# Rotary halves exchanged by ScalarE copies into PSUM instead of signed-permutation matmuls, in a two-layer hybrid encoder

## The reference

```python
def apply_rope(t, cos, sin):
    t1, t2 = jnp.split(tf, 2, axis=-1)          # the two halves of each head, 32 + 32
    return jnp.concatenate([t1 * c - t2 * s, t2 * c + t1 * s], axis=-1)
...
for l in range(DEPTH):
    h = rmsnorm(x, attn_norm_g[l])
    q, k, v, conv_in, gate_logits = jnp.split(h @ w_in[l], SPLITS, axis=-1)
    q, k = apply_rope(q, cos, sin), apply_rope(k, cos, sin)
    y_attn = sliding_window_sink_attention(q, k, v, attn_sinks[l]) @ w_attn_o[l]
    u = causal_dwconv(ca * sigmoid(cb), conv_dw_w[l], conv_dw_b[l])   # width 31
    y_conv = silu(layernorm(u)) @ w_conv_o[l]
    x = x + (sigmoid(g_attn) * y_attn + sigmoid(g_conv) * y_conv) @ w_out[l]
    # then RMSNorm, up-projection, convolution of width 3, SiLU gate, down-projection
```

## Time and profile before

| what | value |
|---|---|
| median of 3 runs | 888.76 us (888.66 to 890.28) |
| profiled execution, its own time | 884.6 us |
| its span, from first to last instruction | 882.8 us |
| TensorE matmul busy | 850.5 us (96%) |
| VectorE busy | 627.9 us (71%) |
| ScalarE busy | 473.2 us (54%) |
| GpSimd busy | 396.5 us (45%) |
| TensorE granted clock, mean | 0.996 of full |

### The profile page before, as it was taken

How to read it: one execution, slowest core, us unless ns; L and a number is a source line. 1 busy time by engine, 2 the same in 40 slices (tenths; PEclk the granted TensorE clock), 3 DMA queues, 4 the chain that set the end, 5 groups by cost and what they waited for, 6 DMA issues and landing times.

```text
span 882.8 us, 16408 instructions
## 1 busy us (share of the span) xinstructions
PE 850.5 (96%) x6800; PEld 825.7 (94%) x6800; DVE 627.9 (71%) x1204; ACT 473.2 (54%) x724; POOL 396.5 (45%) x99
## 2 busy tenths in 40 slices
PE   8899999899999999999989999998999999999996
PEld 8899889799999999999989998897999999999996
DVE  6998899654568875666567688994536787666564
ACT  6544377473555464555663344774635555555452
POOL 4878465467503224222458863655582223322420
PEclk9999999999999999999999999999999999999998
DMA  7654424444454555554435542343544555655521
GB/s 264 205 208 170 143 97 144 143 143 137 151 177 154 195 192 191 192 180 162 148 133 192 191 164 82 137 143 101 173 157 144 183 177 183 206 176 175 192 96 48
DMA packets 22393, 142.32 MB, mean 161 GB/s; under 512 B 2736, under 2 KB 3248, under 8 KB 5808
## 3 DMA queue, kind: packets, MB, share of 16 engines
q1 hardware_dynamic: 21888, 141.02, 46.8%
q10 hardware_dynamic: 432, 0.26, 0.1%
HBM read 140.22 MB, written 1.05 MB: 160 GB/s over the span
## 4 chain that ended last, share of the span: by engine, by line
PE 67%; DVE 23%; ACT 6%; issue 2%; POOL 1%; DMA 1%; SPq 0%; ACTq 0%; DVEq 0%
PE pu L821 17%; PE pu L823 17%; PE pu L822 17%; DVE pc L588 11%; ACT whi L253 3%; DVE wlo L720 2%; PE ps L821 2%; PE ps L822 2%; PE ps L823 2%; PE ps L842 2%; PE po L842 2%; DVE qk L763 2%; POOL wlo L224 1%; DVE top L635 1%; PE pc L822 1%
## 5 line engine op out<-in xcount | busy, mean ns | idle before, releaser
L224 POOL TENSOR_TENSOR wlo<-raw,whi 128x2048 fp32r<-128x2048 f32 x83 | 382.7, 4615 | 447.8 <-ACT whi L253 447.7
L253 ACT ACTIVATE whi<-raw 128x2048 fp32r<-128x2048 f32 x129 | 245.4, 1903 | 19.0 <-PE pu L823 17.8
L821 PE MATMUL pu<-uh,whi 128*128 128x256 f32 x864 | 246.9, 286 | 3.5 <-DVE wlo L720 1.9
L822 PE MATMUL pu<-ul,whi 128*128 128x256 f32 x864 | 244.4, 283 | 0.0
L823 PE MATMUL pu<-uh,wlo 128*128 128x256 f32 x864 | 244.4, 283 | 0.0
L821 PE MATMUL pu<-hh,whi 128*128 128x256 f32 x768 | 222.6, 290 | 10.3 <-POOL wlo L224 5.9
L822 PE MATMUL pu<-hl,whi 128*128 128x256 f32 x768 | 217.8, 284 | 0.0
L823 PE MATMUL pu<-hh,wlo 128*128 128x256 f32 x768 | 217.7, 283 | 0.0
L588 DVE SCALAR_TENSOR_TENSOR pc<-upad,par_all,pc 128x256 f32<-128x256 f32 x464 | 186.4, 481 | 0.3
L821 PEld LDWEIGHTS pu<-uh,whi 128*128 128x128 f32 x864 | 165.7, 192 | 5.5 <-issue 5.1
L822 PEld LDWEIGHTS pu<-ul,whi 128*128 128x128 f32 x864 | 165.7, 192 | 0.2
(11 more groups left out here) (164 smaller groups left out, 1173.9 us busy)
## 6 DMA issues: line engine op xcount, KB each, us to landing
raw<-in_weights SPq DMA_DIRECT2D x129, 1024.0 KB, 4.9
raw<-in_weights SPq DMA_DIRECT2D x12, 256.0 KB, 7.1
x<-in_x_t SPq DMA_DIRECT2D x4, 256.0 KB, 5.0
out_y<-qk SPq DMA_DIRECT2D x4, 256.0 KB, 2.4
par_all<-in_params SPq DMA_DIRECT2D x1, 236.0 KB, 7.3
par_all<-in_params ACTq DMA_DIRECT2D x1, 236.0 KB, 7.0
probs<-in_positions SPq DMA_DIRECT2D x1, 128.0 KB, 7.0
const<-in_const SPq DMA_DIRECT2D x1, 128.0 KB, 7.5
```

The lines of the kernel that those rows point to most:

```text
L224: nc.gpsimd.tensor_tensor(wlo[s][:, :], raw[s][:, :], whi[s][:, :].bitcast(f32), ALU.subtract).then_inc(lo_ready[s], 1)
L253: A(whi[s][:, :], raw[s][:, :], ACT.Copy).then_inc(hi_ready[s], 1)
L821: MM(out, whi[s][:, w], hi, start=start, stop=False, skip_group_check=accumulate)
L822: MM(out, whi[s][:, w], lo, start=False, stop=False, skip_group_check=accumulate)
```

## The change

ScalarE no longer copies q and the k half of `kvraw` to SBUF. It writes the exchanged halves itself, from `pu` to `pt`: four activations for each rotation, each of 32 partitions, reading the block of 32 partitions beside it, with the sign in the scale. The matmuls with `swap`, the constant `swap`, `qraw` and `q_raw` are gone. Each such group on ScalarE waits for `rope_done` of the rotation before it, since `pt` is one tile. VectorE waits for `rot_done` ahead of the multiplication with cos, so that ScalarE and VectorE don't read `pu` at the same time.

```diff
+                def swap_halves(n, src, tiles, scale):
+
+                    if n:
+                        act.wait_ge(rope_done, l * 10 + 2 * n)
+                    for block in range(4):
+                        rows, other = slice(32 * block, 32 * block + 32), slice(32 * (block ^ 1), 32 * (block ^ 1) + 32)
+                        last = A(pt[rows, 0:tiles, :], src[other], ACT.Copy, scale=scale if block % 2 else -scale)
+                    last.then_inc(rot_done, 1)
+
                 u = U_KV
                 act.wait_ge(unit_done[u % RING], finished(l, u))
                 act.wait_ge(u_ready, l * NT + NT)
-                A(kvraw[:, 0, :], pu[u % RING][:, 0, :], ACT.Copy, scale=HEAD_DIM ** -0.5)
+                swap_halves(0, pu[u % RING][:, 0:1, :], 1, HEAD_DIM ** -0.5)
                 A(kvraw[:, 1, :], pu[u % RING][:, 1, :], ACT.Copy).then_inc(kv_raw, 1)
                 next_high(l, u)
                 for i in range(4):
                     u = U_Q + i
                     act.wait_ge(unit_done[u % RING], finished(l, u))
-                    if i >= 2:
-                        act.wait_ge(rope_done, l * 10 + 2 * i)
-                    A(qraw[i % 2], pu[u % RING][:, :, :], ACT.Copy).then_inc(q_raw, 1)
+                    swap_halves(1 + i, pu[u % RING][:, :, :], 2, 1.0)
...
                     if n:
                         dve.wait_ge(rope_done, l * 10 + 2 * n)
+                    dve.wait_ge(rot_done, l * 5 + n + 1)
                     V.scalar_tensor_tensor(a, src, scale, c, ALU.mult, ALU.mult).then_inc(rope_ab, 1)
-                    dve.wait_ge(rot_done, l * 5 + n + 1)
                     V.tensor_tensor(b, b, s, ALU.mult).then_inc(rope_ab, 1)
...
                 for i in range(4):
-                    dve.wait_ge(q_raw, l * 4 + i + 1)
                     rotate(1 + i, pu[(U_Q + i) % RING][:, :, :], 2, 1.0, [qr[:, 2 * i:2 * i + 2, :, odd, :] for odd in range(2)])
...
-                def swap_halves(n, src, tiles):
-
-                    if n:
-                        pe.wait_ge(rope_done, l * 10 + 2 * n)
-                    MM(pt[:, 0:tiles, :], swap, src, start=True, stop=True).then_inc(rot_done, 1)
...
                 pe.wait_ge(kv_raw, l + 1)
-                swap_halves(0, kvraw[:, 0:1, :], 1)
...
                     else:
                         scores(0)
                         standard(U_GATE, hh, hl)
-                    pe.wait_ge(q_raw, l * 4 + i + 1)
-                    swap_halves(1 + i, qraw[i % 2], 2)
                 scores(1)
```

More of the change, by code:

```diff
@@ L39 @@
 NPAR = PA_FW + 2 * FT * 4
-C_FREQ, C_EPS, C_HALFPI, C_GAIN, C_SWAP, C_ID = 0, 1, 2, 4, 20, 148
-NCONST, NEARLY = 276, 20
+C_FREQ, C_EPS, C_HALFPI, C_GAIN, C_ID = 0, 1, 2, 4, 20
+NCONST, NEARLY = 148, 20
 TAPS = CONV_WIDTH
@@ L111, in hybrid_encoder @@
         lnv, rstd = sb("lnv", [P, T]), sb("rstd", [P, T])
-        qraw = [gate[:, 0, 4 + 2 * i:6 + 2 * i, :] for i in range(2)]
         rope_a = gate[:, 1, 4:6, :]
@@ L142, in hybrid_encoder @@
         glu_tanh, u_ready, conv_step = sem("glu_tanh"), sem("u_ready"), sem("conv_step")
-        kv_raw, q_raw, rot_done, rope_ab, rope_done = sem("kv_raw"), sem("q_raw"), sem("rot_done"), sem("rope_ab"), sem("rope_done")
+        kv_raw, rot_done, rope_ab, rope_done = sem("kv_raw"), sem("rot_done"), sem("rope_ab"), sem("rope_done")
         vt_done, v_ready = sem("vt_done"), sem("v_ready")
@@ L862, in _ @@
                 MM(pu[1][:, 0, 0:P], ones[:, :], ones[:, :], start=True, stop=True)
-            swap, ident = const[:, C_SWAP:C_SWAP + P], const[:, C_ID:C_ID + P]
+            ident = const[:, C_ID:C_ID + P]
             for l in range(DEPTH):
@@ L1128 @@
     const[:, C_FREQ] = THETA ** (-(d % 32) / 32.0)
-    const[d ^ 32, C_SWAP + d] = np.where(d % 64 < 32, -1.0, 1.0)
     const[d, C_ID + d] = 1.0
     const[:, C_EPS], const[:, C_HALFPI] = EPS, np.pi / 2
-    const[:, C_GAIN:C_SWAP] = columns(a["attn_norm_g"]).reshape(P, -1)
+    const[:, C_GAIN:C_ID] = columns(a["attn_norm_g"]).reshape(P, -1)
     arrays = {
```

## The result

In the first comparison the changed kernel took 873.23 us (median of 4 runs, 871.62 to 874.73) and the kernel before 888.71 us (884.6 us in its profiled execution). The ratio is 0.9834, 95% interval 0.9807 to 0.9860. The forecast was 877.4 us, its range 875.0 to 882.5: the sign and the way are right, and the gain is larger than the range allowed.

The account below looks back on a forecast made before the run. TensorE was taken to bound the q units and VectorE the attention loop. Gains of 4.6 us (layer 0) and 6.8 us (layer 1) sum to 11.4: 888.76 - 11.4 = 877.4 us, range 875.0 to 882.5.

Parts of the forecast that it names:

- What bounds the kernel: Each layer has two stages: q units bound by TensorE, then the attention loop bound by VectorE's convolution steps.
- Layer 0: All five VectorE waits for the permutation matmul go, VectorE still sets the pace: 4.6 us gained.
- ScalarE's price: Four activations of 512 columns per exchange take 2.1 us, fitting into VectorE's 3.13 us of convolution between rotations.
- Layer 1: VectorE's 5.0 us wait goes, short new ones come, TensorE's lead limits the loop: 6.8 us gained.
- up to 7.6 if the loop's small gaps close too: Upper size of layer 1's gain, equal to VectorE's whole lead at the loop's first maximum.
- the new waits: VectorE in layer 1 waits for ScalarE's exchange 0.65 us at rotation 1 and 0.25 us at rotation 2.
- the 5.76 us that TensorE was to win: Layer 1's loop: 3.87 us from removed matmuls plus waits of 0.87 and 1.02; last exponentials end at 589.1.
- the last two waits of TensorE: At the end of layer 1's loop, 1.24 and 1.57 us shrink so TensorE too comes 6.8 us early.
- only the matmuls come back: Rival: the loop moves with TensorE alone, gaining 7.74 us: 881.0 us; chance 0.14.
- Dearer activations: Rival: 0.9 us per activation exceeds the convolution's cover, gain 6.9 us: 881.9 us; chance 0.12.
- slower: Rival: ScalarE's four activations pace the rotations; at 1.25 us each, 4 us slower: 892.8 us; chance 0.07.
- Against the median: Whole kernel: the 11.4 us sum is taken from the median, 4.2 us above the profiled execution, giving 877.4 us.

Follow-up runs that it names:

- e2: Changed kernel with dead matmuls of the same size put back on TensorE at the permutation matmuls' old places, nothing waiting for them; 880.47 us, ratio 0.9919.
- x4: Kernel before, with each permutation matmul put between the two halves of the unit it stood behind; 883.14 us, ratio 0.9960.
- e3: Changed kernel with four more ScalarE activations of the same shape, into a spare SBUF tile, ahead of the four that count; 889.19 us, ratio 1.0012.
- x6: Changed kernel with unread filler matmuls early in each layer, and VectorE's last-group order changed so values are rounded sooner; 867.11 us, ratio 0.9772.
- a1: Changed kernel run again without edit, the second comparison with the kernel before; 874.44 us against 887.75, ratio 0.9854.
- x5: Kernel before, with unread filler matmuls in TensorE's idle places in the attention loops and early in each layer; 883.61 us, ratio 0.9960.
- c1: Kernel before run again without edit, to read the clock of its repeated executions; 887.55 us against 888.5 beside it.
- e1: Changed kernel with the exchange left out: no permutation matmuls, no wait for them and no activations in their place; 874.13 us, ratio 0.9851.

## Why the prediction was right in its way and wrong in its number

- *What bounds the kernel:* right. The q units were TensorE's, the loop VectorE's. e2 shows that VectorE's waits alone carry some 8 us of the gain, and that TensorE's time adds the rest, 6 to 7 us, on top of them; x4 shows that an earlier matmul with its time kept brings less.
- *Layer 0:* 4.6 us forecast, 4.85 measured. All five waits went, and a cycle of rotation and convolution took 5.90 us (79.09 to 84.98), not 5.96. Unit U_Q+3 and the gate unit found their weights in time; with 4.7 us for an exchange (e3) they didn't.
- *ScalarE's price:* 2.1 us forecast, 2.29 measured; harmless, since 3.03 us were covered.
- *Layer 1:* 6.8 us forecast with "up to 7.6 if the loop's small gaps close too", 7.13 measured. The places and nearly the sizes of the new waits were right. That the first maximum came within 0.1 us of 525.2 is in part luck: rotation 0 began 0.4 us later than reckoned (498.17 against 502.4 - 4.6 = 497.8), and shorter cycles and waits gave 0.4 back. The mis-sized term is the 5.76 us that TensorE was to win up to the last exponentials: they end at 583.84 instead of 594.84, which is 6.15 us beside layer 0's 4.85. A part of it are gaps that the wait rows leave out: ahead of the transposes of group 0, at 543.07, the last matmul starts at 541.92 and takes 0.12 us of its own, so 1.03 us are idle where the row shows 0.87. The rest was not traced. That the last two waits of TensorE (1.24 and 1.57) both shrink was wrong: the first went to 0.26, the second stayed at 1.56, since VectorE needs as long as before from the denominators to the rounding of the values. It is the wait that x6 takes away.
- *The rivals:* "only the matmuls come back" (881.0) would have needed e2 to be no faster than before, and it was 8 us faster. "Dearer activations" and "slower" are excluded by L342's 0.562 us; e3 shows that their mechanism was rightly priced in layer 0, where 4.7 us for an exchange came out at 1.3 us later than before, as reckoned.
- *Against the median: the step that failed.* "The median of the runs is 4.2 us above that execution; against it 888.76 - 11.4 = 877.4 us." This takes the 4.2 us for a constant, the same before and after. It is mostly the cost of stretches at 1.2 GHz behind TensorE's idle places, and the profiled execution was one of those that had least of it: fillers in these places brought the kernel before from 887.75 to 883.61 us, 4.1 less. In the changed kernel the median lay 0.6 us above the profiled execution (873.23 and 872.64), and in a1 2.6 below it (874.44 and 877.04). So it is luck, too, that profile against profile gave 12.0 us: with a1's profiled execution it would have been 884.6 - 877.04 = 7.6. The profile that the forecast was read from had no clock below full in the stages that its rows describe (one stretch early in layer 1, from 456 to 464 us, stands in the changed kernel's profile too), so the sum could hold nothing for it; and the lower end of the range, 12.2 us and 1.6 of spread, gave it nothing either.

What the runs settle about its size: with the idle places filled in both kernels the difference is 12.9 us between medians, 12.1 by the ratios (0.9960 and 0.9824), and 12 between executions with a mean clock of 0.999. The kernel before wins 0.4% (0.2 to 0.6) by the fillers, some 4 us. The changed one wins 0.10% by its first ratio and 0.30% by its second (0.9834 and 0.9854 against 0.9824), 1 to 3 us, on different chips and with intervals that overlap. So, as an estimate, 1 to 3 us of the gain are cost of the lower clock that the changed kernel no longer pays, and 12 to 13 us are its own mechanism. The first comparison came to 15.5 us between medians, the second to 13.3. Whether the changed kernel has fewer such stretches or only covers more of them stays open. The split between the two is no sharper than that. It also stays open how often each stretch recurs.

## What to carry to other kernels

Reckon a change between co-limiting engines as a schedule, with every wait worked out anew from its two arrivals, and not as a list of waits to be struck out: that gave the first maximum of layer 1 to within half a microsecond in each of its parts, and its neglect in x4 missed by 2.6 us (883.14 against 880.5). Before subtracting a sum from a median, compare the clock of the profiled execution with that of others: a kernel whose TensorE idles for one or two microseconds ahead of a full queue can pay again behind it, and here fillers in such places cost nothing (x5). And when a four-fold price sits under cover, measure the cover: here 2.29 us in 3.03 were free, and with 4.7 no gain was left.

## What the runs showed of the hardware

- ScalarE's time went by columns and not by partitions: a copy of 32x512 from PSUM to SBUF took 0.589 us (e3), one of 128x512 0.60. From PSUM to PSUM on other partitions 32x512 took 0.562 us and 32x256 0.347. A run of four starts one each 0.58 us, with no overlap between them; into SBUF the run of four took 2.40 us (e3).
- TensorE's granted clock fell to 1.2 GHz behind idle places of 1.2 and 1.6 us, close together, at the end of a loop, behind one of 2.7 us, and behind single ones of 1.0 us (c1 at 564 us, e1 at 122 us) and 1.8 us (x5 at 19 us), in some executions of the same program and not in others. Behind the one of 3.2 us early in layer 1 it fell in all ten profiled executions that have no filler there.
- With matmuls in such places (x5) the mean clock of an execution lay at 0.996 to 0.999, where the kernel before had 0.984 to 0.996, and its time at 882.64 to 884.96 us instead of 884.06 to 891.88.
